# Pairing two heads' scores in banded and sparse attention, and placing filler products behind every second step

## The reference

```python
def token_mixer(h, ...):
    z = h @ w_in                      # all projections and the gates
    y_a = dsa_attention(...)          # A: an indexer picks 128 keys per query; 8 heads, 2 KV heads, ALiBi
    y_b = rglru_branch(...)           # B: conv, gates, scan
    y_c = mla_attention(...)          # C: latent attention, 8 heads, rotary key, causal, 128-query blocks
    y_d = sliding_window_attention(...)  # D: window 128, 8 heads, 2 KV heads, sinks, ALiBi
    proj = einsum('bsnw,nwd->bsnd', stack([y_a, y_b, y_c, y_d]), w_branch)
    return sum(sigmoid(gates) * proj, axis=n) @ w_out
```

## Time and profile before

| | |
|---|---|
| median of three runs | 3069.15 us |
| the profiled execution's own time | 3071.67 us |
| its span, first to last instruction | 3069.9 us |
| mean granted TensorE clock over the span | 0.986 |
| TensorE busy | 2938.7 us, 96% of the span |
| VectorE busy | 1609.0 us, 52% |
| ScalarE busy | 1024.6 us, 33% |
| GpSimd busy | 167.6 us, 5% |

### The profile page before, as it was taken

How to read it: one execution, slowest core, us unless ns; L and a number is a source line. 1 busy time by engine, 2 the same in 40 slices (tenths; PEclk the granted TensorE clock), 3 DMA queues, 4 the chain that set the end, 5 groups by cost and what they waited for, 6 DMA issues and landing times.

```text
span 3069.9 us, 38852 instructions
## 1 busy us (share of the span) xinstructions
PE 2938.7 (96%) x12968; PEld 2299.1 (75%) x12968; DVE 1609.0 (52%) x2596; ACT 1024.6 (33%) x1693; POOL 167.6 (5%) x131
## 2 busy tenths in 40 slices
PE   5999999999999999999989999999999999999997
PEld 3888867777777877888768888667777778688885
DVE  6655346666445636532266552566655365465323
ACT  2322224444434323222232222344434343232221
POOL 0111010000000001110011100100000000111100
PEclk9999999999999999999989999999999999999999
DMA  5654322111112215533245552221111123164232
GB/s 231 218 205 154 134 70 75 49 49 56 63 42 96 97 55 173 189 96 100 65 140 190 192 184 83 71 62 49 56 56 60 65 76 103 35 218 165 96 101 71
DMA packets 89148, 329.16 MB, mean 107 GB/s; under 512 B 10017, under 2 KB 10401, under 8 KB 87586
## 3 DMA queue, kind: packets, MB, share of 16 engines
q1 hardware_dynamic: 88994, 327.25, 31.5%
HBM read 325.11 MB, written 2.10 MB: 107 GB/s over the span
## 4 chain that ended last, share of the span: by engine, by line
issue 66%; PE 32%; POOL 2%; DVE 1%; ACT 0%; DVEq 0%; POOLq 0%; ACTq 0%
PE bank L429 10%; PE bank L430 10%; PE bank L431 10%; POOL x L538 1%; POOL rstd_tok L531 1%; PE bank L1525 0%; DVEq L1186 0%; DVE diag L1122 0%; DVE h_low L1133 0%; DVE norm_tmp L1138 0%; ACT h_high L778 0%; DVE x L1187 0%; DVE ffn_act L1275 0%; ACT ffn_high L824 0%; DVE norm_tmp L1183 0%
## 5 line engine op out<-in xcount | busy, mean ns | idle before, releaser
L429 PE MATMUL bank<-h_high,w_high 128*128 128x512 f32 x2384 | 954.3, 400 | 8.8 <-DVE h_low L1133 8.7
L413 DVE TENSOR_TENSOR w_low<-w_raw,w_high 128x1024 fp32r<-128x1024 f32 x440 | 568.0, 1291 | 700.4 <-ACT w_high L407 699.4
L431 PE MATMUL bank<-h_high,w_low 128*128 128x512 f32 x2384 | 934.8, 392 | 0.0
L430 PE MATMUL bank<-h_low,w_high 128*128 128x512 f32 x2384 | 934.3, 392 | 0.0
L407 ACT ACTIVATE w_high<-w_raw 128x1024 fp32r<-128x1024 f32 x440 | 462.3, 1051 | 399.0 <-PE bank L431 397.5
L429 PEld LDWEIGHTS bank<-h_high,w_high 128*128 128x128 f32 x2384 | 452.3, 190 | 115.1 <-DVE h_low L1133 16.9
L431 PEld LDWEIGHTS bank<-h_high,w_low 128*128 128x128 f32 x2384 | 451.1, 189 | 96.9
L430 PEld LDWEIGHTS bank<-h_low,w_high 128*128 128x128 f32 x2384 | 452.1, 190 | 92.3 <-issue 2.5
L429 PE MATMUL bank<-ffn_high,w_high 128*128 128x512 f32 x704 | 280.4, 398 | 0.0
L431 PE MATMUL bank<-ffn_high,w_low 128*128 128x512 f32 x704 | 274.2, 389 | 0.0
L430 PE MATMUL bank<-ffn_low,w_high 128*128 128x512 f32 x704 | 274.1, 389 | 0.0
(11 more groups left out here) (191 smaller groups left out, 2804.4 us busy)
## 6 DMA issues: line engine op xcount, KB each, us to landing
w_raw<-stream SPq DMA_DIRECT2D x444, 512.0 KB, 3.6
ada_raw<-ada SPq DMA_DIRECT2D x144, 512.0 KB, 3.7
ada_start<-ada SPq DMA_DIRECT2D x8, 1024.0 KB, 19.4
mixer_consts<-mixc SPq DMA_DIRECT2D x2, 1152.0 KB, 5.1
x<-x_in SPq DMA_DIRECT2D x1, 2048.0 KB, 9.7
silu_c<-silu_row SPq DMA_DIRECT2D x4, 512.0 KB, 4.2
out<-x SPq DMA_DIRECT2D x8, 256.0 KB, 2.2
lru_w<-lruw SPq DMA_DIRECT2D x2, 512.0 KB, 3.6
```

Source lines behind the costliest of these rows:

```text
L413: eng.tensor_tensor(wL[:, slot], raw[:, slot], wH[:, slot].bitcast(F32), ALU.subtract).then_inc(lo_ready[slot].sem, 1)
L429: eng.matmul(o, a, rhs_h, start=first, stop=False)
L430: eng.matmul(o, a, rhs_l, start=False, stop=False)
L431: return eng.matmul(o, b, rhs_h, start=False, stop=last)
```

## The change

Three edits, one in the list and two in the attention of D and A.

- Filler products are placed only behind odd steps (C, D and A). Behind an odd step there are now one or two halves, behind an even step none. Top-k rounds stay behind every step as before.
- In D and A the heads of a block are taken in the order 0, 4, 1, 5, 2, 6, 3, 7. At an even step TensorE waits until all earlier shifts are done, and then computes the scores of this step and the next, one from partitions 0 to 63 and one from partitions 64 to 127, into banks 4 and 5. At an odd step it computes no scores.
- VectorE makes both biases and both shifts at the even step, ahead of that step's multiplication to `y_tok`, and none at the odd step. C keeps one score and one shift per step.

```diff
-            while fill and (nf - len(fill)) * STEPS_ALL < (st + 1) * nf:
+            while st % 2 and fill and (nf - len(fill)) * STEPS_ALL < (st + 1) * nf:
                 yield fill.pop(0)
...
+HEAD_AT = {"C": range(HEADS), "D": (0, 4, 1, 5, 2, 6, 3, 7), "A": (0, 4, 1, 5, 2, 6, 3, 7)}
...
-            b, h = st // HEADS, st % HEADS
+            b, h = st // HEADS, HEAD_AT[br][st % HEADS]
...
-            if st < STEPS:
-                g = att_index(br, st)
-                b, h, k0, nk = keys(br, st)
+            ahead = [st] if br == "C" else [st, st + 1] if st % 2 == 0 else []
+            for st1 in ahead if st < STEPS else ():
+                g = att_index(br, st1)
+                b, h, k0, nk = keys(br, st1)
...
-                if g >= 2:
-                    pe.wait_ge(shifted.sem, shifted.at(l, g - 1))
                 q = slice(b * P, (b + 1) * P)
                 kk = slice(k0 * P, (k0 + nk) * P)
                 if br == "C":
-                    a, c = qC[0:96, h, q], kC[0:96, h, kk]
-                else:
-                    rows = slice(64 * (h // 4), 64 * (h // 4) + 64)
+                    if g >= 2:
+                        pe.wait_ge(shifted.sem, shifted.at(l, g - 1))
+                    pe.matmul(bank[4 + g % 2][:, 0:P * nk], qC[0:96, h, q], kC[0:96, h, kk], start=True, stop=True
+                              ).then_inc(scores_ready.sem, 1)
+                elif st % 2 == 0:
+
+                    pe.wait_ge(shifted.sem, shifted.at(l, g))
                     qq, kx = (aq, ak) if br == "A" else (dq, dk)
-                    a, c = qq[rows, h % 4, q], kx[rows, kk]
-                pe.matmul(bank[4 + g % 2][:, 0:P * nk], a, c, start=True, stop=True).then_inc(scores_ready.sem, 1)
+                    for i in range(2):
+                        rows = slice(64 * i, 64 * i + 64)
+                        pe.matmul(bank[4 + (g + i) % 2][:, 0:P * nk], qq[rows, h, q], kx[rows, kk], start=True,
+                                  stop=True).then_inc(scores_ready.sem, 1)
```

## The result

| | kernel before | changed kernel |
|---|---|---|
| median, five runs of each | 3069.15 us (3066.48 to 3076.84) | 3093.48 us (3089.18 to 3101.77) |
| ratio, with its 95% interval | 1 | 1.008 (1.0059 to 1.0101) |
| profiled execution, span | 3071.67, 3069.9 us | 3092.38, 3090.6 us |
| mean granted clock | 0.986 | 0.981 |
| TensorE busy | 2938.7 us, 96% | 2911.3 us, 94% |

The change makes the kernel 0.8% slower. TensorE is busy for 27 us less, and the span is 20.7 us longer. A line of the old source at L1480 (scores) is L1485 now, L1490 (transpositions) is L1496, L1502 (value products) is L1508, L1097 (`y_tok`) is L1099; the filler's three products are L430 to L432.

What follows compares the result with a forecast made beforehand. TensorE, busy for 96% of the span, was taken as the bound. -50.8 + 14.2 + 32.8 + 13.3 = +9.5 us on 3071.67 gave 3081.2, less 2.5 for the median: 3079 us, range 3048 to 3094.

Steps and rivals of the forecast that it cites:

- the forecast's own case: Whole kernel: scores saved, but waits and clock cost more; 3079 us, chance 0.54.
- Scores: D and A: each pair's second score is free and switching saves a little; TensorE's work falls by 50.8 us.
- Wait 1: Inside each pair of steps: the odd step's transposition waits for ScalarE's eviction; 7.1 us per layer, 14.2 in all.
- Wait 2, D and A: Block ends: the next block's first value product waits for `y_tok` without filler; A 9.5, D 11.0 us per layer.
- Wait 2, C: C's block ends, without filler at steps 10 and 18: waits of 2.5 and 0.5 us, 3.0 per layer.
- Clock: Granted clock falls to 0.5 behind 16 long idle times of TensorE, 1.66 us each: 13.3 us more, bounds 0 and 25.
- Outside attention: Rest of the kernel: nothing else moves, no DMA is added, ring units keep order and mean rate; no cost.
- the waits are shorter: Block ends: VectorE has time, so waits for `y_tok` are shorter; 3053 us, or 3032 if nearly all covered; chance 0.30 together.
- Pairs don't overlap fully: Scores in D and A: one pass more per pair, 21 us; 3100 us, chance 0.04.
- VectorE bounds D: D: VectorE is late at every step, so transpositions wait for exponentials; 4 us more per layer, 3087 us, chance 0.12.
- the placement: Filler behind odd steps only: in C it moves by one step at most, costing and gaining nothing but the waits.

Runs made afterwards that it cites:

- e5: The changed kernel with heads in natural order, so both scores of a pair lie in the same 64 partitions: 3117.37 us, ratio 1.0142.
- e6: The changed kernel with the multiplication to `y_tok` between the even step's two shifts instead of behind both: 3067.84 us, ratio 0.9985.
- e2: The kernel before with filler behind odd steps only, one score and one shift per step: 3102.57 us, ratio 1.0100.
- e8: The changed kernel with 2 to 5 unused products ahead of the waits for `y_tok` at block ends of D and A: 3072.99 us, ratio 1.0003.
- e3: The changed kernel with filler behind even steps instead of odd ones, the remainder behind the last step: 3011.03 us, ratio 0.9806.
- e11: The kernel before with filler behind even steps only, one score and one shift per step: 3044.04 us, ratio 0.9912.

## Why the prediction was right, point by point

Forecast slower, at 3079 us, in a range of 3048 to 3094; it is slower, at 3093.48. The direction and the mechanism were right, and the size was too small: +9.5 us forecast for the profiled execution, +20.7 measured. That the measurement lies in the range is in part luck: it is 0.5 us inside, beyond the 3066 to 3092 that the forecast's own case had, and inside only since the range was widened for another rival. By its steps, for both layers:

| term | forecast | measured in the trace of after |
|---|---|---|
| a second score in the pair | nothing | nothing: x4 in 0.70 and 1.13 us, as x2 |
| wait inside pairs of steps | +14.2 | some +20.6 |
| waits at block ends | 28.1 per layer, net +32.8 | 30.4 per layer, net some +37.4 |
| clock, over the whole span | +13.3 | +14.4 |
| outside the attention | 0 | +3.9 by length: moved filler, and clock |
| sum of these over the forecast | | +12.1; the span has +11.2 |

- **Scores, -50.8.** The pair is free, as the earlier trace rows had it. TensorE's busy time fell by 27.4 us only, because more of what is left ran at half clock (61.4 us of the attention's time, 27.3 before). With that taken out (14.4, below) it fell by 41.8, and its idle time grew by 48.1. The forecast's -50.8 counts by starts, where the waits come out some 10 us longer than by idle time (58.0 against 48.1), so both counts give a net of 6 to 7 us. By the Trainium skill ("TensorE: Matmul & The Clock Gate", section "The mechanism") starts and ends keep strictly to program order. Pass by pass, that is not what these rows show: four passes in program order can't take the 0.70 us of two. The four records of the pair at 712.33 start at 712.326, 712.333, 712.646 and 712.653, and the trace marks a product as finished on the last two only: the second head's first pass runs beside the first head's first. Product by product the order is kept; the rule failed as I applied it, pass by pass. e5 is how it looks where the passes do follow each other, 0.43 us longer.
- **Wait 1, mis-sized.** By starts, the odd transposition is late by 0.45 us with 128 keys, 0.34 with 256, 0.22 with 384 and 0.10 with 512, where I had 0.35, 0.24, 0.12 and 0. I let the transposition start 0.05 us behind the end of ScalarE's eviction; it is 0.15 (713.81 to 713.96). 0.1 us in each of 64 pairs is 6.4 us.
- **Wait 2, D and A.** Forecast against measured, by distances between starts, for steps 10, 18, 26: D 3.2, 4.4, 3.4 against 3.6, 4.3, 3.1; A 2.0, 2.2, 5.3 against 2.0, 2.7, 4.5. With steps 34 and 35 the sums are 13.8 against 13.7 and 10.4 against 10.4. The count of what stands ahead of `y_tok` on VectorE carried this, and e6, which takes one item out of it, confirms it. That the sums agree so closely is luck: single waits are off by up to 0.8 us, and their errors cancel.
- **Wait 2, C, mis-sized.** 3.9 per layer forecast, with step 34, and 6.3 measured: step 18 waits 2.2 us, and I took 0.5 out of bounds of 0.5 to 2.5. C's rows show the chain that e2 shows and that my sum didn't have: the odd step's exponential (to 598.77 on ScalarE), the unit's high part, its low part, the shift, `y_tok`, with the even step's score at 598.92. ScalarE, then VectorE:

```profile
598.77 1.04 ACT L408 ACTIVATE w_high<-w_raw 128x1024 fp32r<-128x1024 f32 x1
```

```profile
599.85 1.22 DVE L414 TENSOR_TENSOR w_low<-w_raw,w_high 128x1024 fp32r<-128x1024 f32 x1 [0.33 <-ACT w_high L408]
602.65 0.69 DVE L1099 TENSOR_TENSOR y_tok<-bank,recip 128x512 f32<-128x512 f32 x1 [0.59 <-issue]
```

- **Clock, near.** By the rounded clocks, D and A lose twice (0.07 x 125.6 + 0.05 x 150.5), 32.6 us, where the four stretches had 13.3. That counts some of the holes twice: in the stall at step 19 the clock falls 2 us after the last matmul, and the first 2 us at 0.5 have no matmul in them (721.60 in the last section). Counted as half of TensorE's busy time at half clock, over the whole span, it is 28.7 us before and 43.1 now: +14.4, which is +15.8 in the attention and -1.4 outside. The way there was not shown by rows: I counted 16 idle times at 1.66 us each, where C's idle times of 1.74 and 2.01 us left the clock whole, and the one of 4.04 in D cost more.
- **Outside attention.** The 3.9 us are two things that partly cancel. A half of 2.8 us per layer has left A for the stretch behind it, 5.6 us in all, which costs nothing. The clock accounts for the rest: it gives back 3.2 us between and behind the layers, and takes the 1.7 ahead of C. There the code is not touched, and from 500 us to C's first score both kernels run the same 190 matmuls, but in one stretch this execution had half clock:

```profile
530.50:533.90 3.40, 3.40 (x9) 2.64 (x10) 2.43 (x4) 1.39 (x2) 0.00 (x0) 0.50 0.00 0
```

  The same stretch before, 530.30 to 533.70, has 17 matmuls at 1.00. That is a difference between executions, not of the change: e8 has the changed kernel's code there, and C's first score at 551.0 as the kernel before. The clock term of a single profile is uncertain by such amounts.
- **How it closes.** -50.8 for the scores, +20.6 and +37.4 for the waits and +14.4 for the clock is 21.6, and the span grew by 20.7. What the forecast lacked was 6.4 us inside the pairs, 4.6 at block ends and 1.1 of clock.

Of the rivals, *the waits are shorter* is out: the six waits average 3.4 us, over the 2.6 from which it decides. *Pairs don't overlap fully* is out by the pair's own rows. *VectorE bounds D* was not the case in the changed kernel, whose lost time is at block ends, but VectorE does hold up D in e3: moving 16 top-k rounds out of D gave 7.3 us there, clock included.

The step of the prediction that I would redo is the placement. I weighed the loss of filler at block ends rightly, and did not ask about the half of the rule that I took for neutral: e11 shows that filler behind even steps alone, without any pair, gains 27 us, more than half of what the pairs remove.

## What to carry to other kernels

In this kernel, filler work on the engine that bounds it isn't best spread evenly; it belongs behind the step whose result another engine must hand back, here the even steps, since the lag of 10 steps and the block of 8 make every handing over even. Moving it by one step was worth 82 us (e3 against the changed kernel), with the same instructions. A pairing that saves work on one engine moves work together on another: list what now stands ahead of the instruction that the first engine waits for, and the waits can be worked out, here to within 0.8 us in D and A. In C, where the chain through ScalarE was left out, one was off by 1.7. And two edits that share a wait are tried one at a time, since the pairs alone were a gain of 1.1% that the placement hid.

## What the runs showed of the hardware

- Two score products whose operands lie in partitions 0 to 63 and 64 to 127 cost what one costs: 0.70 us for four records of 64x256, and 1.13 for four of 64x512. In the same 64 partitions the second costs 0.43 us with 256 keys (e5), less than the 0.63 from a lone one to the next operation.
- Behind idle times of TensorE of 3.4 and 4.0 us the granted clock is 0.5. In the changed kernel, behind the stall that ends at 693.84, and in and behind the one that ends at 723.60 (from 719.60 to 721.60, also without a matmul, it is still 1.00):

```profile
694.30:697.70 3.40, 3.40 (x12) 2.83 (x12) 2.42 (x5) 1.54 (x2) 0.00 (x0) 0.51 0.00 0
721.60:723.60 2.00, 0.00 (x0) 0.03 (x1) 1.58 (x5) 1.30 (x5) 0.00 (x0) 0.51 0.07 29
723.60:728.40 4.80, 4.80 (x16) 4.12 (x17) 3.37 (x5) 1.55 (x2) 0.00 (x0) 0.50 0.00 0
```

- Products that nobody needs, put into these holes, gave back 20.5 us (e8). They filled 36 us of idle time (34.7 to 16.7 per layer), so a stall costs what it lasts and here about half as much again in clock; after an idle time of 2.01 us in C it cost nothing more.
- From the end of a ScalarE eviction to TensorE's start on it is 0.15 us (713.81 to 713.96). Small as it is, 64 times 0.15 is 9.6 us.
